# Base copies behind the weight loads, splits in another order in the first and last retention heads, and one vector's modulation summed as a stationary operand

## The chip, the cores and the metric

The kernel runs on one core of one Trainium2 chip. The metric is the device time of one execution in microseconds, as the median of the runs. Five engines work beside each other on the core: PE (TensorE, matrix products), DVE (VectorE), ACT (ScalarE), POOL (GpSimd) and SP (SyncE, which here only issues DMAs). Each engine takes its own instructions in the order in which they were written, and semaphores tie the engines together.

## The reference, cut to what matters

Two layers work on 512 latent tokens of width 1024, behind 256 context tokens. Layer 0 mixes the tokens with a gated MLP, layer 1 with bidirectional retention in four heads. Each is followed by a squared-ReLU MLP of width 4096. Every sub-layer is modulated by scale, shift and gate vectors, which are one product of a conditioning vector with `ada_w[i]`:

```python
mod_l = silu(c) @ ada_w[i] + ada_b[i]           # six vectors: sh1, s1, g1, sh2, s2, g2
h = x * (1 + s) + sh                            # per sub-layer
x = layernorm(alpha * x + g * f(h))

# layer 1's f: four heads, each with q, k, v and two gates from h @ b_w_in
s = gmlp; o_f, o_b = retention forward, retention backward (rope on q and k)
y = headnorm(o_f) * silu(g_f) + headnorm(o_b) * silu(g_b)
f(h) = y @ w_out
# the MLP: f(h) = square(relu(h @ w1)) @ w2
```

## The kernel before

**Precision and units.** The data is fp32. PE multiplies it as a sum of a high and a low part, with three matmuls per product (`hi*hi`, `lo*hi`, `hi*lo`; in the rows they are L1143, L1144, L1145, or L1181 to L1183 in the heads). Weights come in units of 128x1024 (512 KB). SP loads a unit into one of four `raw` slots (L911). ACT copies it to the high part (`split_hi`: L1799, L1842). DVE subtracts that from the unit to get the low part (`split_lo`: L2325, L2456). Then PE uses both. SP's load into a slot waits until DVE's split of the unit that lay in the slot is done (`done(n)`, a wait on `lo_done`), so a split that comes later on DVE also makes a later load.

**Phases.** Layer 0's mixer is followed by its MLP: ffn0a, six trips of ffn0 (p = 0 to 5), and ffn0z, the last piece. Then come the layer norm ln0b, three heads (`heads`), the last head (`headz`), ln1a, and the MLP of layer 1 (ffn1a, ffn1, ffn1z), which ends with ln1b. The MLPs and the heads' gate products use sums of weight blocks (`T1` to `T4`). For a head they are made in DRAM: SP copies a block there (`base`, L941, 1 MB each), and POOL adds another to it with an accumulating DMA (`gate_sum`, L3499). T2 adds T1's sum, so it waits for that; T4 adds T2's.

**The end of ffn0z.** While PE does the last blocks of the MLP, SP issues the lnbc loads, the four base copies for head 0, and the raw loads of the first head's units 0 to 3. ACT splits units 0 and 1, and then copies `rows` out of PSUM (`mod_rows`, L1945). `rows` is the sum over partitions of the modulation's products (`macc`), which the DVE accumulated: `mod_sums` (L1335) sums it with four matmuls of `ones`, and gives rows; `mod_columns` (L1345) transposes the copied rows with three matmuls, and DVE adds the bias (`mod1_columns`). PE can't go past `mod_columns` before ACT's copy is done. The gate row is then stored to DRAM from `modc` (L827) and loaded again (L834), and the raw loads for head 0's next units stand behind that on SP. POOL adds the MLP's blocks to the residual (L3409), and then shifts it with four accumulating DMAs (`shift_by_dma0`, L3451).

**The first head.** Beside its own units it makes the sums of the activations for the gate products: DVE `gx` (`operand1_sum`, L3136 and others), ACT the high parts `s_gs`, `pa_hi`, `s_y`, `pa_lo` (`operand1_hi`, L2146), DVE the low parts (`operand1_lo`, L3142). ACT's first of them also waits for POOL's four shifts. PE needs the units 6 and 7 split meanwhile.

**The end of headz.** Four `y` blocks (t = 3 to 0) are normed on DVE (L2369 to L3345), transposed on PE (L1636), copied by ACT as a high part (L2263) and by DVE as a low part (`y_low`, L3323), and multiplied with the units OUT to OUT+3. DVE then adds each product to the residual (L2692). The units of ffn1a's start are split in the same stretch (its unit 1 is `in_v`, its unit 2 `in_scr`).

## Time and profile before

| | us |
|---|---|
| median of 3 runs | 1962.84 |
| lowest and highest run | 1961.87, 1963.0 |
| the profiled execution | 1963.9 |
| its span in the trace | 1962.1 |
| PE busy | 1929.5 (98% of the span) |
| DVE busy | 1368.7 (70%) |
| ACT busy | 673.4 (34%) |
| POOL busy | 384.8 (20%) |

The mean granted clock of PE over the span is 0.995 of full speed. Busy times overlap; only the time in which PE has nothing to do, or runs slower, can be taken off without removing matmuls. In the views below a timeline row is start, duration, engine, line, operation, `out<-in`, and in brackets the idle time before it with what ended it.

### The profile page before, as it was taken

The numbers are of one execution on the slowest core, as the hardware profiler recorded it, in microseconds if no ns is written. First come the engines' busy times: TensorE is split into PE (matmuls) and PEld (weight loads), VectorE is DVE, ScalarE is ACT, GpSimd is POOL, SyncE is SP. The second block draws the span as 40 slices with busy tenths as digits, with TensorE's granted clock in tenths as the row PEclk, the third lists the DMA queues.
The fourth block names the chain that finished last, engine by engine and source line by source line (L and its number), as shares of the span: only waits on it lengthen the run. The fifth ranks groups of instructions, "written<-read, shape, count | busy, mean of one in ns | idle before, by whom it ended". The sixth has DMA issues, their size and how long they took to land.

```text
span 1962.1 us, 24859 instructions
## 1 busy us (share of the span) xinstructions
PE 1929.5 (98%) x9429; PEld 1651.9 (84%) x9429; DVE 1368.7 (70%) x1972; ACT 673.4 (34%) x930; POOL 384.8 (20%) x364
## 2 busy tenths in 40 slices
PE   9999999999999999999699999999999999999998
PEld 6889889889889988899587888888888878888887
DVE  3756678688778776777577744753754687777778
ACT  3423222234323322232246324423423444444443
POOL 0400311322221222112320130030030026100004
PEclk9999999999999999999899999999999999999999
DMA  9613334235998999988666366446447425886646
GB/s 329 256 65 75 109 122 129 94 119 150 204 250 208 222 225 220 241 229 209 191 155 218 127 200 194 155 158 205 169 133 240 161 86 172 236 220 188 181 143 149
DMA packets 120275, 350.07 MB, mean 178 GB/s; under 512 B 17504, under 2 KB 30432, under 8 KB 115424
## 3 DMA queue, kind: packets, MB, share of 16 engines
q1 hardware_dynamic: 91056, 267.58, 39.5%
q0 software_dynamic: 27280, 77.08, 21.8%
q10 hardware_dynamic: 1824, 3.85, 0.6%
q8 instruction: 75, 1.23, 0.3%
q14 instruction: 40, 0.33, 0.1%
HBM read 295.49 MB, written 39.87 MB: 171 GB/s over the span
## 4 chain that ended last, share of the span: by engine, by line
PE 89%; DVE 4%; DMA 3%; issue 1%; ACT 1%; POOL 1%; SPq 0%; POOLq 0%; DVEq 0%; ACTq 0%
PE bank L1143 17%; PE bank L1145 17%; PE bank L1144 17%; PE bank L1181 4%; PE bank L1183 3%; PE bank L1182 3%; PE bank L1544 3%; PE bank L1547 3%; PE bank L1546 3%; PE bank L1591 2%; PE bank L1594 2%; PE bank L1593 2%; PE bank L1776 2%; PE bank L1775 2%; PE bank L1773 2%; DMA raw<-w_units_d 2%
## 5 line engine op out<-in xcount | busy, mean ns | idle before, releaser
L2325 DVE TENSOR_TENSOR w_lo<-raw,w_hi 128x1024 fp32r<-128x1024 f32 x132 | 168.8, 1281 | 190.2 <-ACT w_hi L1799 189.9
L1799 ACT ACTIVATE w_hi<-raw 128x1024 fp32r<-128x1024 f32 x132 | 139.2, 1055 | 296.6 <-PE bank L1145 159.7
L1143 PE MATMUL bank<-w_hi,act_hi 128*128 128x512 f32 x504 | 198.3, 394 | 0.0
L1145 PE MATMUL bank<-w_hi,act_lo 128*128 128x512 f32 x504 | 196.5, 390 | 0.0
L1144 PE MATMUL bank<-w_lo,act_hi 128*128 128x512 f32 x504 | 196.3, 390 | 0.0
L1143 PE MATMUL bank<-hT_hi,w_hi 128*128 128x384 f32 (+2 forms) x544 | 192.2, 353 | 0.0
L1144 PE MATMUL bank<-hT_lo,w_hi 128*128 128x384 f32 (+2 forms) x544 | 190.9, 351 | 0.0
L1145 PE MATMUL bank<-hT_hi,w_lo 128*128 128x384 f32 (+2 forms) x544 | 190.8, 351 | 0.0
L1181 PE MATMUL bank<-w_hi,hT_hi 128*128 128x512 f32 x336 | 131.3, 391 | 2.0 <-DVE w_lo L2325 2.0
L3382 POOL TENSOR_TENSOR rstd<-veps,tiny 128x1 f32<-128x1 f32 x58 | 38.7, 666 | 471.6 <-DVE veps L2378 471.6
L1182 PE MATMUL bank<-w_lo,hT_hi 128*128 128x512 f32 x336 | 130.8, 389 | 0.0
L1183 PE MATMUL bank<-w_hi,hT_lo 128*128 128x512 f32 x336 | 130.8, 389 | 0.0
L3392 POOL TENSOR_TENSOR res_lat<-res_lat,gy 128x512 f32<-128x512 f32 x56 | 78.6, 1430 | 207.7 <-DVE gy L2434 207.6
L1143 PEld LDWEIGHTS bank<-w_hi,act_hi 128*128 128x128 f32 x504 | 94.6, 188 | 24.4 <-issue 5.4
L1145 PEld LDWEIGHTS bank<-w_hi,act_lo 128*128 128x128 f32 x504 | 94.6, 188 | 20.0
L1144 PEld LDWEIGHTS bank<-w_lo,act_hi 128*128 128x128 f32 x504 | 94.7, 188 | 18.9
L1143 PEld LDWEIGHTS bank<-hT_hi,w_hi 128*128 128x128 f32 x544 | 102.4, 188 | 9.0 <-issue 0.2
L1144 PEld LDWEIGHTS bank<-hT_lo,w_hi 128*128 128x128 f32 x544 | 102.4, 188 | 8.9 <-issue 0.2
L1145 PEld LDWEIGHTS bank<-hT_hi,w_lo 128*128 128x128 f32 x544 | 102.3, 188 | 8.4
L1842 ACT ACTIVATE w_hi<-raw 128x1024 fp32r<-128x1024 f32 x46 | 48.6, 1056 | 134.1 <-PE bank L1145 116.6
L1807 ACT ACTIVATE act_hi<-stage 128x384 fp32r<-128x384 f32 x96 | 50.4, 526 | 115.6 <-DVE stage L2518 61.3
L2456 DVE TENSOR_TENSOR w_lo<-raw,w_hi 128x1024 fp32r<-128x1024 f32 x46 | 56.2, 1222 | 36.9 <-ACT w_hi L1842 36.9
(447 smaller groups left out, 4859.7 us busy)
## 6 DMA issues: line engine op xcount, KB each, us to landing
raw<-w_units_d SPq DMA_DIRECT2D x234, 512.0 KB, 4.6
mod<-mod_units_d SPq DMA_DIRECT2D x64, 384.0 KB, 4.4
wsum<-w_units_d SPq DMA_DIRECT2D x45, 512.0 KB, 4.6
raw<-weight_sums_d SPq DMA_DIRECT2D x32, 512.0 KB, 4.3
wsum<-w_units_d POOLq DMA_DIRECT2D x26, 512.0 KB, 8.3
wsum<-wsum POOLq DMA_DIRECT2D x19, 512.0 KB, 6.9
bv<-mod_units_d SPq DMA_DIRECT2D x16, 512.0 KB, 3.7
weight_sums_d<-w_units_d POOLq DMA_DIRECT2D x8, 1024.0 KB, 14.3
```

Source lines behind the costliest of these rows:

```text
L1143: nc.tensor.matmul(out, s_hi, m_hi, start=first, stop=False)
L1144: nc.tensor.matmul(out, s_hi, m_lo, start=False, stop=False)
L1145: return nc.tensor.matmul(out, s_lo, m_hi, start=False, stop=last)
L1181: nc.tensor.matmul(bank[t][:, :], hT_hi[:, kc, tt], hi[:, c], start=kc == 0, stop=False)
L1182: nc.tensor.matmul(bank[t][:, :], hT_hi[:, kc, tt], lo[:, c], start=False, stop=False)
L1183: last = nc.tensor.matmul(bank[t][:, :], hT_lo[:, kc, tt], hi[:, c], start=False, stop=kc == KC - 1)
L1544: nc.tensor.matmul(out, hi[:, w], x_hi[:, kc, :], start=opens and kc == 0, stop=False, skip_group_check=True)
L1546: nc.tensor.matmul(out, hi[:, w], x_lo[:, kc, :], start=False, stop=False, skip_group_check=True)
L1547: last = nc.tensor.matmul(out, lo[:, w], x_hi[:, kc, :], start=False, stop=kc == KC // 2 - 1, skip_group_check=True)
L1799: nc.scalar.activation(halves_of(phase, k, i)[0], raw[:, s, :], ACT.Copy).then_inc(hi_done, 1)
L2325: tt(lo, raw[:, s, :], f32(hi), ALU.subtract).then_inc(lo_done, 1)
L3392: gt(r, r, gy[:, e % 2, :], ALU.add).then_inc(res_added, 1)
```

## The change

It has four parts.

1. **Order on SP and POOL at the end of ffn0z.** The four base copies are issued behind the raw loads of units 0 to 3 and not ahead of them, and POOL's sums T1 and T3 stand behind the additions to the residual.
2. **Columns at once.** For the trips p = 3, 4 and 5 of ffn0, `column_sums` takes a 128x128 block of `macc` as the stationary operand and two columns of ones as the moving one, three matmuls for each of two blocks. The result is already a column, so the four matmuls of `mod_sums` and the three transposes are left out. ACT copies 6 columns in place of 384, and DVE adds two halves.
3. **The first head.** Units 6 and 7 are split earlier among the activation sums, on ACT and DVE.
4. **The last head.** DVE splits OUT to OUT+2 between the `y` blocks and not in one run ahead of the gates, OUT+3 and ffn1a's unit 0 behind the last `y` block. ACT's copies are reordered to match.

```diff
                     sp.wait_ge(pe_step, step_of("ffn0z", 0, "q3.1"))
                     load_lnbc(lnbc0, 2)
-                    for x, block in ((T1, "B11"), (T3, "B12"), (T2, "B22"), (T4, "B21")):
-                        base(0, x, block)
                 done(7)
                 if more:
...
                 else:
                     load(at + 8 + 3, 3)
+                    for x, block in ((T1, "B11"), (T3, "B12"), (T2, "B22"), (T4, "B21")):
+                        base(0, x, block)
                 mods(4)
                 mods(5)
...
 
+                def column_sums(label, b, block):
+
+                    free(phase, i, label)
+                    for j in range(3):
+                        at = (3 * block + j) * P
+                        last = nc.tensor.matmul(bank[b][:, 2 * j:2 * j + 2], sum1(p)[:, at:at + P], ones[:, 0:2],
+                                                start=True, stop=True)
+                    last.then_inc(pe_step, 1)
+
                 def rows():
                     pe.wait_ge(mod_used, len(MOD1_SEQ) if phase == "ffn0z" else MOD1_SEQ.index((p, KC - 1)) + 1)
+                    if phase == "ffn0" and p >= PIECES_MIXED:
+                        column_sums("rows0", 6, 0)
+                        return
                     mod_sums(phase, i, "rows0", 6, [sum1(p), sum1(PIECES_F - 1 if phase == "ffn0z" else p, 1)],
                              WIDE_M1 // 2)
...
                     block0_hi(p, 10)
                     block0_hi(p + 1, 0)
-                    mod_rows(phase, i, 0, rows1[:, :], 6, begin)
+                    if p > PIECES_MIXED:
+                        act.wait_ge(dve_drain, drained(phase, i - 1, "cols0")[1])
+                    mod_rows(phase, i, 0, rows1[:, 0:6] if p >= PIECES_MIXED else rows1[:, :], 6, begin)
                     block0_hi(p + 1, 1)
                 else:
                     act.wait_ge(stage_full, count("full", phase, i, 2 + d))
                     stage_split(phase, i, 4 + d, k_hi[:, d, 0:TOKL], TOKL)
                 for k in range(6, 9):
-                    if first and k < 8:
-                        operand1_hi(2 * k - 12)
-                        operand1_hi(2 * k - 11)
+                    if first:
+                        for n in ((0,), (1,), (2, 3))[k - 6]:
+                            operand1_hi(n)
                     split_hi(phase, i, k, used_unit(phase, i, k - 2))
 
                 act.wait_ge(dec_in, h * 16 + 48)
...
                 if phase == "heads":
                     split_hi(phase, i, OUT, used_unit(phase, i, OUT - 2))
                 else:
-                    for k in range(OUT, OUT + 3):
-                        split_hi(phase, i, k, step_of(phase, i, "g2.1"))
-                    split_hi(phase, i, OUT + 3, used_unit(phase, i, OUT - 2))
+                    split_hi(phase, i, OUT, step_of(phase, i, "g2.1"))
                 gate(2, "g4.0")
                 gate(3, "g4.1")
                 if phase == "heads":
                     split_hi(phase, i, OUT + 1, used_unit(phase, i, OUT - 1))
                 else:
-                    split_hi("ffn1a", 0, 0, used_unit(phase, i, OUT - 1))
+                    for k in range(OUT + 1, OUT + 3):
+                        split_hi(phase, i, k, step_of(phase, i, "g2.1"))
+                    split_hi(phase, i, OUT + 3, used_unit(phase, i, OUT - 2))
                 for t in reversed(range(LAT)):
                     act.wait_ge(pe_step, step_of(phase, i, f"y{t}"))
                     nc.scalar.activation(act_hi1[:, :, t * P:(t + 1) * P],
                                          bank[4 + t][:, :].rearrange("p (a b) -> p a b", a=CH), ACT.Copy)\
                         .then_inc(psum_hi, 1)
+                    if phase == "headz" and t == 3:
+                        split_hi("ffn1a", 0, 0, used_unit(phase, i, OUT - 1))
                     if phase == "headz" and t == 1:
                         split_hi("ffn1a", 0, 1, step_of(phase, i, "ob0"))
                 if phase == "headz":
...
-            EARLY = {"gmlpz": ("ffn0a", 0, 1), "ffn0z": ("heads", 0, 2), "headz": ("ffn1a", 0, 2)}
+            EARLY = {"gmlpz": ("ffn0a", 0, 1), "ffn0z": ("heads", 0, 2), "headz": ("ffn1a", 0, 1)}
...
+                    if phase == "headz" and n == 1:
+                        split_lo("ffn1a", 0, 2)
                     if n < LAT + 1:
                         drain_block(phase, 2 * n, order)
                     second_half(phase, n - 1, ln_phase)
...
+                    if i >= PIECES_MIXED:
+                        dve.wait_ge(act_drain, drained(phase, i, "rows0")[1])
+                        tt(out[:, 0], rows1[:, 0:6].rearrange("p (j v) -> p j v", v=2), bias[:, 0], ALU.add)
+                        tt(out[:, 1], bank[7][:, 0:6].rearrange("p (j v) -> p j v", v=2), bias[:, 1], ALU.add)\
+                            .then_inc(dve_drain, 1)
+                        return
                     src = bank[7][:, 0:3 * P].rearrange("p (j b v r) -> p b j v r", j=3, b=2, v=2)
...
                 for d in range(2):
                     stage_lo_part(phase, i, 4 + d, k_lo[:, d, 0:TOKL], k_hi[:, d, 0:TOKL], TOKL)
-                if first:
-
-                    operand1_sum(gx21, gx11, gx21)
                 split_lo(phase, i, 6)
                 if first:
+
+                    operand1_sum(gx21, gx11, gx21)
                     operand1_lo(0)
                     operand1_lo(1)
+                    split_lo(phase, i, 7)
 
                     operand1_sum(gx11, gx22, gx11)
 
...
@@ -3308,15 +3336,10 @@
                 gate_c22(1)
                 decayed(1, 12, 10, backward, range(3, 6),
                         {3: (lambda: of_gated(2),), 4: (13, lambda: of_gated(3))})
-                if phase == "headz":
-                    for k in range(OUT, OUT + 3):
-                        split_lo(phase, i, k)
                 gate_c21(0)
                 gate_c21(1)
-                if phase == "headz":
-                    split_lo(phase, i, OUT + 3)
-                else:
-                    split_lo(phase, i, OUT)
+                split_lo(phase, i, OUT)
+                if phase == "heads":
                     split_lo(phase, i, OUT + 1)
                 def y_low(t):
                     dve.wait_ge(psum_hi, h * 10 + (TILES0 + LAT - t))
@@ -3344,10 +3367,13 @@
                     dve.wait_ge(dve_drain, drained(phase, i, f"ob{t}")[1])
                     stt(y[:, t, :], rbuf[:, n % 2, :], rstd[:, 4 + t:5 + t], y[:, t, :], ALU.mult, ALU.add)\
                         .then_inc(y_step, 1)
-                    if phase == "headz" and t == 3:
-                        split_lo("ffn1a", 0, 0)
+                    if phase == "headz":
+                        if t > 1:
+                            split_lo(phase, i, OUT + LAT - t)
+                        elif not t:
+                            split_lo(phase, i, OUT + 3)
                 if phase == "headz":
-                    split_lo("ffn1a", 0, 1)
+                    split_lo("ffn1a", 0, 0)
                 y_low(0)
...
                 nc.gpsimd.dma_start(weight_sums_d[h, x], other, accum_op=ALU.add, max_dma_last_dim=8192)\
                     .then_inc(t_sum0[x], 16)
 
-            gate_sum(0, T1)
-            gate_sum(0, T3)
             for t in range(TILES0):
                 pool.wait_ge(gy_added[t], 16 * 2 * (PIECES_F - 1))
             add_blocks("ffn0z", "ln0b", 2 * TILES0)
-            gate_sum(0, T2)
+            for x in (T1, T3, T2):
+                gate_sum(0, x)
             shift_by_dma0("ln0b", LAT)
             gate_sum(0, T4)
             pool.wait_ge(shifted0, 16 * (TILES0 + LAT))
```

**SP, at the end of ffn0z.** `raw` is a weight slot, `weight_sums_d` the four base copies. Before:

```order
179 L838 DMA lnbc<-ln_d 128x1024
180 L839 DMA lnbc<-ln_d 128x1024
181 L941 DMA weight_sums_d<-w_units_d 16x16384 x4
182 L911 DMA raw<-w_units_d 128x1024 x4
183 L1004 DMA rope<-rope_d 128x1024
184 L827 DMA gate_rows_d<-modc 128x8x1 x2
```

After the change:

```order
179 L838 DMA lnbc<-ln_d 128x1024
180 L839 DMA lnbc<-ln_d 128x1024
181 L911 DMA raw<-w_units_d 128x1024 x4
182 L941 DMA weight_sums_d<-w_units_d 16x16384 x4
183 L1004 DMA rope<-rope_d 128x1024
184 L827 DMA gate_rows_d<-modc 128x8x1 x2
```

The four raw loads stand ahead of the four base copies; the rope load and the store of the gate row stay behind both.

**DVE, in the first head.** The first row is the split of the head's keys, `w_lo` are the units 6, 7 and 8. Before:

```order
793 L2334 TENSOR_TENSOR k_lo<-stage,k_hi 128x512 x2
794 L3136 TENSOR_TENSOR gx<-gx 128x1024
795 L2325 TENSOR_TENSOR w_lo<-raw,w_hi 128x1024
796 L3142 TENSOR_TENSOR s_gs<-gx,s_gs 128x1024
797 L3142 TENSOR_TENSOR pa_hi<-gx,pa_hi 128x1024
798 L3136 TENSOR_TENSOR gx<-gx 128x1024
799 L3204 TENSOR_TENSOR gx<-gx,hT_hi 128x1024
800 L3206 TENSOR_TENSOR gx<-gx,hT_lo 128x1024
801 L2325 TENSOR_TENSOR w_lo<-raw,w_hi 128x1024
802 L3142 TENSOR_TENSOR s_y<-gx,s_y 128x1024
803 L3142 TENSOR_TENSOR pa_lo<-gx,pa_lo 128x1024
804 L2325 TENSOR_TENSOR w_lo<-raw,w_hi 128x1024
```

After the change:

```order
796 L2354 TENSOR_TENSOR k_lo<-stage,k_hi 128x512 x2
797 L2345 TENSOR_TENSOR w_lo<-raw,w_hi 128x1024
798 L3164 TENSOR_TENSOR gx<-gx 128x1024
799 L3170 TENSOR_TENSOR s_gs<-gx,s_gs 128x1024
800 L3170 TENSOR_TENSOR pa_hi<-gx,pa_hi 128x1024
801 L2345 TENSOR_TENSOR w_lo<-raw,w_hi 128x1024
802 L3164 TENSOR_TENSOR gx<-gx 128x1024
803 L3232 TENSOR_TENSOR gx<-gx,hT_hi 128x1024
804 L3234 TENSOR_TENSOR gx<-gx,hT_lo 128x1024
805 L3170 TENSOR_TENSOR s_y<-gx,s_y 128x1024
806 L3170 TENSOR_TENSOR pa_lo<-gx,pa_lo 128x1024
807 L2345 TENSOR_TENSOR w_lo<-raw,w_hi 128x1024
```

Unit 6 is split ahead of the first `gx`, and unit 7 ahead of the last three.

**ACT, at the end of headz.** `xw_hi` are the units OUT to OUT+2, the next `w_hi` is OUT+3, then come ffn1a's unit 0 (`w_hi`), unit 1 (`in_v_hi`) and unit 2 (`in_scr_hi`), and the four copies of `y` (`pa_hi<-bank`). Before:

```order
577 L2214 ACTIVATE gs<-bank 128x512 x2
578 L1799 ACTIVATE xw_hi<-raw 128x1024 x3
579 L1799 ACTIVATE w_hi<-raw 128x1024
580 L2209 ACTIVATE gs<-gs 128x512 x2
581 L1799 ACTIVATE w_hi<-raw 128x1024
582 L2263 ACTIVATE pa_hi<-bank 128x4x128 x3
583 L1799 ACTIVATE in_v_hi<-raw 128x1024
584 L2263 ACTIVATE pa_hi<-bank 128x4x128
585 L1799 ACTIVATE in_scr_hi<-raw 128x1024
```

After the change:

```order
578 L2232 ACTIVATE gs<-bank 128x512 x2
579 L1814 ACTIVATE xw_hi<-raw 128x1024
580 L2227 ACTIVATE gs<-gs 128x512 x2
581 L1814 ACTIVATE xw_hi<-raw 128x1024 x2
582 L1814 ACTIVATE w_hi<-raw 128x1024
583 L2281 ACTIVATE pa_hi<-bank 128x4x128
584 L1814 ACTIVATE w_hi<-raw 128x1024
585 L2281 ACTIVATE pa_hi<-bank 128x4x128 x2
586 L1814 ACTIVATE in_v_hi<-raw 128x1024
587 L2281 ACTIVATE pa_hi<-bank 128x4x128
588 L1814 ACTIVATE in_scr_hi<-raw 128x1024
```

Only OUT is copied ahead of the gates; ffn1a's unit 0 is behind the first copy of `y`, its unit 1 still ahead of the last copy of `y`.

## Rows read from the trace of the kernel before

**Rows 1.** What PE waited for, whole span: us in total, times, longest

```profile
PE bank L1345 <- ACT rows L1945: 16.6, 1, 16.6
PE bank L1636 <- DVE y L3345: 2.4, 2, 1.9
```

**Rows 2.** Timeline of PE around the wait at the end of ffn0z

```profile
943.65 0.39 PE L1145 MATMUL bank<-xw_hi,act_lo 128*128 128x512 f32 x1
960.67 0.90 PE L1345 MATMUL bank<-ident,rows 128*128 128x128 f32 x3 [16.63 <-ACT rows L1945]
...
982.94 1.10 PE L1363 MATMUL bank<-ident,res_lat 128*128 128x128 f32 x8
```

**Rows 3.** A window in the wait: length, busy of each engine (instructions), clock, DMA share, GB/s

```profile
950.00:960.00 10.00, 0.00 (x0) 0.00 (x0) 1.23 (x1) 1.87 (x2) 0.00 (x0) 0.50 1.01 282
```

**Rows 4.** Timeline of PE, the same program stretch in gmlpz

```profile
426.94 0.60 PE L1345 MATMUL bank<-ident,vtok 128*128 128x128 f32 x4
...
446.71 1.09 PE L1363 MATMUL bank<-ident,res_lat 128*128 128x128 f32 x8
```

**Rows 5.** Timeline of ACT at the end of the wait

```profile
959.18 1.06 ACT L1799 ACTIVATE in_s_hi<-raw 128x1024 fp32r<-128x1024 f32 x1 [4.54 <-DMA raw<-w_units_d]
960.15 0.47 ACT L1945 ACTIVATE rows<-bank 128x384 f32<-128x384 f32 x1
```

**Rows 6.** Timeline of SP's DMA issues

```profile
929.70 2.51 SPq L941 DMA_DIRECT2D weight_sums_d<-w_units_d  x4
933.16 8.31 SPq L911 DMA_DIRECT2D raw<-w_units_d  x4
...
964.30 1.06 SPq L827 DMA_DIRECT2D gate_rows_d<-modc  x2
980.86 0.33 SPq L834 DMA_DIRECT2D gate_lat<-gate_rows_d  x1
...
1040.51 0.38 SPq L1028 DMA_DIRECT2D raw<-weight_sums_d  x1
```

**Rows 7.** Landing times of the four raw loads issued from 933.2 to 941.1

```profile
DMA to landing us min/median/max: 20.4/20.7/22.3
```

**Rows 8.** Page, section 6: KB each, us to landing

```profile
raw<-w_units_d SPq DMA_DIRECT2D x234, 512.0 KB, 4.6
```

**Rows 9.** Landing times of the raw load issued at 1569.7

```profile
DMA to landing us min/median/max: 3.5/3.5/3.5
```

**Rows 10.** Landing times of weight_sums_d DMAs issued from 925 to 945

```profile
DMA to landing us min/median/max: 7.3/13.8/18.3
```

**Rows 11.** Timeline of PE around trip 3's sums and transposes

```profile
767.95 0.85 PE L1335 MATMUL bank<-macc,ones 128*32 128x384 f32 x8
...
771.60 0.49 PE L1345 MATMUL bank<-ident,rows 128*128 128x128 f32 x3
```

**Rows 12.** Timeline of PE at the start: dcol stationary, two columns moving

```profile
46.01 0.95 PE L1325 MATMUL bank<-dcol,rbuf 128*128 128x2 f32 x8
```

**Rows 13.** Timeline of PE in the first head

```profile
1037.85 0.50 PE L1181 MATMUL bank<-w_hi,hT_hi 128*128 128x512 f32 x1 [1.30 <-DVE w_lo L2325]
...
1047.06 0.50 PE L1181 MATMUL bank<-w_hi,hT_hi 128*128 128x512 f32 x1 [0.72 <-DVE w_lo L2325]
```

**Rows 14.** Timeline of ACT in the first head

```profile
1032.54 1.04 ACT L2146 ACTIVATE s_gs<-gx 128x1024 fp32r<-128x1024 f32 x1
```

**Rows 15.** Timeline of DVE at the end of headz

```profile
1598.46 0.74 DVE L3345 SCALAR_TENSOR_TENSOR y<-rbuf,rstd,y 128x512 f32<-128x512 f32 x1
```

**Rows 16.** Timeline of ACT at the end of headz

```profile
1596.13 1.05 ACT L1799 ACTIVATE in_v_hi<-raw 128x1024 fp32r<-128x1024 f32 x1
```

**Rows 17.** Timeline of PE at the end of headz

```profile
1615.84 1.09 PE L1363 MATMUL bank<-ident,res_lat 128*128 128x128 f32 x8
```

**Rows 18.** Timeline of POOL: T2's sum, the fourth shift of the residual

```profile
993.80 0.96 POOL L3499 DMA_DIRECT2D weight_sums_d<-weight_sums_d  x1
...
1026.32 0.86 POOL L3451 DMA_DIRECT2D res_lat<-lnbc  x1 [10.15 <-issue]
```

More of the change, by code:

```diff
@@ L1556, in columns @@
                 def columns():
+                    if phase == "ffn0" and p >= PIECES_MIXED:
+                        column_sums("cols0", 7, 1)
+                        return
                     mod_columns(phase, i, 0, rows1, 7)
@@ L1898, in ffn0 @@
                     split_hi("heads", 0, 1, step_of(phase, i, "q3.1"))
+                    act.wait_ge(dve_drain, drained("ffn0", p - 1, "cols0")[1])
                     mod_rows(phase, i, 0, rows1[:, :], 6, begin)
@@ L3012, in mod1_columns @@
                     bias = bias.unsqueeze(3).to_broadcast([P, 2, 3, 2])
+                    if i >= PIECES_MIXED:
[3 more added lines that the diff above has]
+                            .then_inc(dve_drain, 1)
+                        return
                     src = bank[7][:, 0:3 * P].rearrange("p (j b v r) -> p b j v r", j=3, b=2, v=2)
@@ L3192, in head @@
                     stage_lo_part(phase, i, 4 + d, k_lo[:, d, 0:TOKL], k_hi[:, d, 0:TOKL], TOKL)
+                split_lo(phase, i, 6)
                 if first:
                     operand1_sum(gx21, gx11, gx21)
-                split_lo(phase, i, 6)
-                if first:
                     operand1_lo(0)
                     operand1_lo(1)
+                    split_lo(phase, i, 7)
                     operand1_sum(gx11, gx22, gx11)
@@ L3206, in head @@
                     tt(kcs(gx22[:, :]), kcs(gx22[:, :]), f32(hT_lo[:, second, g_first]), ALU.add).then_inc(s_sum0, 1)
-                split_lo(phase, i, 7)
-                if first:
                     operand1_lo(2)
                     operand1_lo(3)
+                else:
+                    split_lo(phase, i, 7)
                 split_lo(phase, i, GATE)
```

## The prediction

> **What bounds the kernel now.** I read first what PE waited for over the whole span [rows 1], because PE is busy almost throughout and little else can be won. One wait stands out: 16.6 us, once, in front of the transposes of `rows` (L1345), released by ACT's copy. The next two are small: 2.4 us in two waits for `y` in the last head (the longer 1.9), and two waits for a low split in the first head are 1.30 and 0.72 us [rows 13].
>
> Then the timeline around the large wait [rows 2]. The last matmul before it starts at 943.65 and the transposes at 960.67, which is 17.02 us from start to start, where the matmuls before stood 0.23 us apart: 16.8 us are lost. The window in the wait [rows 3] shows PE at nothing, DVE with a single 1.23 us instruction, ACT at 1.87 us, and the DMA engines fully in use (share 1.01, 282 GB/s): the engines wait for transfers. It shows the granted clock at 0.50, which is 1.2 of 2.4 GHz, and the matmuls go on at that for a while after the wait. What this costs can be read from two stretches with the same program, the down blocks up to the first transposes of the residual: here 982.94 - 960.67 = 22.27 us [rows 2], in gmlpz 446.71 - 426.94 = 19.77 us [rows 4]. The difference, 2.5 us, belongs to the wait too.
>
> What is the copy late for? ACT copies `rows` at 960.15, right behind its split `in_s_hi` of unit 1, and that had waited 4.54 us for its `raw` load and started at 959.18 [rows 5]. SP shows why the load landed so late [rows 6]: four base copies of 1 MB were issued at 929.70 and the raw loads from 933.16 on, so that unit 1 lay behind 4 MB. Those four raw loads landed 20.4 to 22.3 us after their issue [rows 7]. The raw loads of the whole kernel land in a median of 4.6 us [rows 8], one alone in 3.5 us [rows 9]. The base copies and the sums made from them took from 7.3 to 18.3 us [rows 10], and nobody on SP needs a sum before 1040.51 [rows 6].
>
> **Part 1, the order on SP and POOL.** The raw loads are now issued ahead of the base copies. SP issues the four from 933.16 over 8.31 us [rows 6], held only by the slots; so that of unit 1 goes out at about 937 and lands at 941 (3.5 us) to 942 (4.6 us). Unit 0 is there before ACT gets to it. ACT then splits unit 1 in 1.06 us and copies `rows` in 0.47 us [rows 5]: done at about 943.2, where PE wants it at 943.65 + 0.23 = 943.88. The wait goes, with 0.7 us to spare, and with it the slow clock: 16.8 + 2.5 = 19.3 us. Against it I set 0.3 us: the DVE split that ran inside the wait [rows 3] now falls among the drains of the down blocks (nothing at best, its whole 1.23 us at worst). **Gain 19.0 us.**
>
> What is late next? Each step behind the base copies on SP's queue. The rope load and the stores of the gate row stand behind them in order. Before, the stores were issued at 964.30 and the load that waits for them went out at 980.86 [rows 6], 16.6 us later. After, they are issued some 17 us earlier, but find the base copies still under way; I put them in DRAM at 971 to 973, which is 8 to 10 us earlier than before while PE is 19 us earlier, so 9 to 11 us of slack are used up. The gate row is needed only by the head's gated sums, some 20 us on, and the next four raw loads behind it on SP are for units 4 and on. I take this as covered; if the cover is gone, each microsecond costs one. POOL's sums T1 and T3 go behind its additions, and T2 behind them, from 993.80 [rows 18] - 19.3 = 974.5 on: even at 18.3 us each [rows 10] T1, then T2, land by about 1011, and SP's first use stands at 1040.51 - 19.3 = 1021 [rows 6]. Hidden.
>
> **Part 2, the columns.** Three trips lose four summing matmuls (8 records, 0.85 us) and three transposes (0.49 us), 1.34 us [rows 11], and get two times three matmuls with two moving columns. The nearest row is that of `dcol` with two columns, 8 records in 0.95 us [rows 12]; so six records cost 0.71 us, twice 1.43 us. That is 0.09 us more per trip, **a loss of 0.2 us** in all. At the price of a transpose, 0.49 / 3 = 0.16 us [rows 11], the six cost 0.98 and 1.1 us are gained; at the price of a whole `dcol` group for each half, 1.90, 1.7 us are lost. The smaller copy on ACT and the second addition on DVE are not on the path in ffn0: PE stands there for neither [rows 1].
>
> **Part 3, the first head.** PE waited for the low splits of units 6 and 7 at 1037.85 (1.30 us) and 1047.06 (0.72 us) [rows 13]; both waits are followed by a slow first matmul (0.50 us), and from start to start I count 1.46 and 0.88 us lost. ACT's `s_gs` copy starts at 1032.54 [rows 14], and unit 6's split stands behind the next copy, which itself waits for a `gx`. With unit 6 directly behind `s_gs`, ACT has it at 1034.6 and DVE's low part, 1.23 us as in [rows 3], is there at 1035.8, where PE is ready at 1037.85 - 1.46 = 1036.4. Unit 7 is split before the last three `gx` operations and is ready at about 1040.4, over 4 us ahead of need. The sums that are pushed back by one split each are used after unit 8. **Gain 2.3 us**; 0 if the margin of 0.6 us is used up by something else.
>
> **Part 4, the last head.** The three low splits ahead of the gates go between the `y` blocks; so the waits for `y`, 2.4 us in all [rows 1], should go. But the low split of OUT+3 now stands behind the last `y` block on DVE. Before, that block's end was at 1598.46 + 0.74 = 1599.2 [rows 15]; without the waits it is at about 1596.8. Then come the split (1.2 us), only then SP's load of ffn1a's unit 1 (3.5 us, [rows 9]), and ACT's `in_v_hi` (1.05 us, [rows 16]), which stands ahead of the last copy of `y` on ACT: 1596.8 + 1.2 + 3.5 + 1.05 = 1602.6. Before, `in_v_hi` was already split at 1596.13 and that copy could start at 1599.2 + 0.6 = 1599.8. So the last copy comes 2.8 us later, the products ahead of it on PE 2.4 us earlier. Before, the stretch ended with the transposes at 1615.84 [rows 17]; it ends between 2.4 us earlier and 2.8 us later. The two nearly cancel: **a loss of 0.3 us**.
>
> **The sum** is -19.0 + 0.2 - 2.3 + 0.3 = -20.8 us. Durations come from the execution of 1963.9 us, which would become 1943.1; it lies 1.1 us above the median of 1962.84, and the median becomes 1942.0 us.
>
> **Rivals.** *(a) Only part of the wait goes.* The raw loads still meet the first base copies on the engines. If unit 1's took what loaded transfers took, 7.3 us at the least and 13.8 in the median [rows 10], it landed at 944.3 or 950.8, the copy of `rows` 1.6 us later, and PE waited 2.0 or 8.5 us. With up to 1.5 us of slow clock that leaves a total of 18.8 or 10.8 us: 1944 to 1952, in the middle 1948. The 4.6 us of the other loads [rows 8] speak against it.
>
> *(b) The transfers aren't ordered.* If the base copies and the raw loads share the engines whatever their order of issue, unit 1 lands as before and only the small parts are left: -1.8 us, 1961.0, no change that can be told. Against it: the raw loads behind the base copies took 20.4 us or more [rows 7], those elsewhere 4.6 [rows 8].
>
> *(c) POOL's sums hold up its shifts.* T2's issue waits for T1, and the four shifts stand behind it. T1 is issued where T2 was at 993.80 [rows 18], less 19.3: 974.5 + 18.3 = 993 lets the first shift out just where it would be, and the fourth, at 1026.32 before [rows 18], is due at 1007. If sums took twice as long beside busy engines (36.6 us), T2 went out at 1011, the fourth shift at 1016 instead of 1007, and ACT's `s_gs` in the first head, which waits for it, would hold unit 6 back by about 8 us: total 13 us, 1950. For it: two sums of the base copies took up to 18.3 us while DVE stood nearly still [rows 10], so a busy DVE has not been seen with them there.
>
> The Trainium skill ("DMA: Bandwidth & Descriptors", section SWDGE vs HWDGE vs iDMA) speaks for it: the descriptor rings of DMAs that GpSimd issues lie in SBUF, where DVE can lock GpSimd out in its two-port mode. No run here shows such a lock. By it the time would be that of (c).
>
> *(d) Slower.* The same mechanism carried further: the gain is eaten up when T2 lands so late that the first head's sum unit comes 20.8 us late, that is after 1021 + 20.8 = 1042, and slower by 0.2% from 1046. T1 and T2 issued from 974.5 would have to take 71 us together; at 18.3 us each they take 37 [rows 10].
>
> *(e) The last head goes one way.* If the load of ffn1a's unit 1 lands in 4.6 us or more, the copy of the last `y` is later still: +2.5 in place of +0.3, total 18.6, 1944.2. If PE's products ahead cover all of it, -2.4: total 23.5, 1939.3.
>
> **How the numbers follow.** The forecast with (e) on both sides has 0.80, (a) 0.06, (c) 0.06, (b) 0.04, (d) 0.02, and 0.02 is for a gain beyond 24 us. A measurement of this kernel tells about 0.2%, 3.9 us, from no change. Faster: 0.80 + 0.06 + 0.06 + 0.02 = 0.94; same: (b), 0.04; slower: (d), 0.02. The range reaches from (e)'s better end, 1939.3, less 0.5 us for the spread of the runs, to the middle of (a), and leaves out half of (a), (b), (c), (d) and the larger gain, less than 0.2 in all: 1938.8 to 1948.0.
>
> **What would show it.** Right: no wait at L1345 in ffn0z, a granted clock of 1.00 through that stretch, raw loads landing in 3 to 5 us there, 19.8 us from the column transposes to the residual's first transposes; no wait for units 6 and 7; in headz no wait for `y`, but one for the last `y_low`, with ACT's `in_v_hi` waiting for DMA. Wrong: a new PE wait in the first head with ACT's `s_gs` released by a DMA, or DVE waiting for the gate row. The step most likely to be off in size is part 4.

## The result, and the profile after

The changed kernel takes 1943.64 us (median of 6 runs, 1941.41 to 1946.51), the kernel before 1963.42 us (6 runs, 1961.87 to 1966.47). The ratio is 0.9899, with a 95% interval of [0.9886, 0.9912]: 19.8 us faster, where 20.8 were forecast. The profiled execution took 1941.41 us, its span is 1939.6 us, and it is the fastest of the six.

The waits of PE in the changed kernel, over the whole span, answer to [rows 1]:

```profile
PE bank L1363 <- ACT res_lat L1976: 2.0, 1, 2.0
PE bank L1143 <- DVE pa_lo L3346: 1.8, 2, 1.4
PE bank L1317 <- DMA mod<-mod_units_d: 1.5, 4, 0.6
PE bank L1418 <- POOL tiny L3489: 1.3, 1, 1.3
```

The wait for `rows` (16.6 us) and those for `y` are gone, and no wait for a low split in the first head is left. Two new ones are in the last head: for the low part of `y` (`pa_lo`) and for the normed residual (`res_lat`). The other two rows stood in the kernel before too, with 0.5 and 1.3 us. The next view is PE's timeline at the places of [rows 2], the transposes of `rows` and the first transposes of the residual:

```profile
942.48 0.49 PE L1345 MATMUL bank<-ident,rows 128*128 128x128 f32 x3
...
962.16 1.09 PE L1363 MATMUL bank<-ident,res_lat 128*128 128x128 f32 x8
```

These are 19.68 us apart, where they were 22.27. The window over the former wait answers to [rows 3]; its columns are the same:

```profile
940.00:950.00 10.00, 10.00 (x47) 8.28 (x46) 8.46 (x15) 4.50 (x5) 6.05 (x5) 1.00 1.10 406
950.00:960.00 10.00, 10.00 (x46) 8.29 (x45) 7.57 (x18) 2.49 (x2) 7.95 (x8) 1.00 0.69 158
```

PE is at 10.00 of 10.00 us and the granted clock at 1.00. SP and ACT show why, as in [rows 5] and [rows 6]. First SP's issues, then ACT:

```profile
931.79 8.32 SPq L911 DMA_DIRECT2D raw<-w_units_d  x4
940.15 2.55 SPq L941 DMA_DIRECT2D weight_sums_d<-w_units_d  x4
...
945.07 7.39 SPq L827 DMA_DIRECT2D gate_rows_d<-modc  x2
968.04 0.33 SPq L834 DMA_DIRECT2D gate_lat<-gate_rows_d  x1
```

```profile
938.95 1.06 ACT L1814 ACTIVATE in_s_hi<-raw 128x1024 fp32r<-128x1024 f32 x1
939.92 0.47 ACT L1963 ACTIVATE rows<-bank 128x384 f32<-128x384 f32 x1
```

The four raw loads, which landed 20.4 to 22.3 us after their issue [rows 7], landed in

```profile
DMA to landing us min/median/max: 3.4/3.5/4.3
```

ACT's `in_s_hi` has no wait ahead of it, and the copy of `rows` is done at 939.92 + 0.47 = 940.4, 2.1 us before PE gets to the transposes.

To see where the time went in each part, I compared the start of the same PE instruction in the two traces:

| PE instruction | before | after | difference |
|---|---|---|---|
| behind the column step of trip 5 | 898.26 | 896.59 | -1.67 |
| transposes of `rows` in ffn0z | 960.67 | 942.48 | -18.19 |
| first transposes of the residual | 982.94 | 962.16 | -20.78 |
| unit 6 of the first head | 1037.85 | 1015.62 | -22.23 |
| unit 7 of the first head | 1047.06 | 1023.78 | -23.28 |
| transposes of y3 in headz | 1587.70 | 1563.69 | -24.01 |
| transposes of y1 | 1594.98 | 1568.70 | -26.28 |
| first product with the last y | 1604.69 | 1580.19 | -24.50 |
| transposes of the residual | 1615.84 | 1593.34 | -22.50 |

The first 1.7 us belong to no part of the change: 0.7 us arise in the first 35 us and 1.0 us at one wait at 532.8, in code that it does not touch, and such steps of either sign stand in every trace below. The end of ffn0z gives 19.4 us (the difference just ahead of it was -1.38), the first head 2.5, and headz first 3.0 and then takes 3.8 back. That is 21.1 us in this pair of executions, of which the medians of all runs show 19.8.

### The profile page after: what moved, and what is told of

It is laid out like the page before. It is cut to its first block, busy times and chain, and to the rows that moved or that the text cites. A ratio compares the mean times of both kernels' runs of the same rounds, so it can differ in the third digit from the quotient of the medians.

```text
span 1939.6 us, 24868 instructions
## 1 busy us (share of the span) xinstructions
PE 1924.6 (99%) x9432; PEld 1652.1 (85%) x9432; DVE 1368.7 (71%) x1975; ACT 672.5 (35%) x930; POOL 382.8 (20%) x364
## 3 DMA queue, kind: packets, MB, share of 16 engines
q8 instruction: 75, 1.23, 0.2%
## 4 chain that ended last, share of the span: by engine, by line
PE 92%; DVE 2%; DMA 2%; issue 1%; POOL 1%; SPq 1%; ACT 1%; POOLq 0%; DVEq 0%; ACTq 0%
PE bank L1143 17%; PE bank L1144 17%; PE bank L1145 17%; PE bank L1181 4%; PE bank L1182 4%; PE bank L1183 4%; PE bank L1544 3%; PE bank L1547 3%; PE bank L1546 3%; PE bank L1608 3%; PE bank L1609 3%; PE bank L1606 3%; PE bank L1790 2%; PE bank L1788 2%; PE bank L1791 2%
## 5 line engine op out<-in xcount | busy, mean ns | idle before, releaser
L1181 PE MATMUL bank<-w_hi,hT_hi 128*128 128x512 f32 x336 | 131.0, 390 | 0.0
L1144 PEld LDWEIGHTS bank<-w_lo,act_hi 128*128 128x128 f32 x504 | 94.7, 188 | 18.8
```

The lines of the kernel that those rows point to most:

```text
L1144: nc.tensor.matmul(out, s_hi, m_lo, start=False, stop=False)
L1181: nc.tensor.matmul(bank[t][:, :], hT_hi[:, kc, tt], hi[:, c], start=kc == 0, stop=False)
```

## The experiments

Each time is a median, each ratio is against runs of the kernel before on the same chip, and what a run gains or loses is worked out from its ratio. "In the trace" means by the starts of the same PE instructions, as in the table above.

**One part at a time.** *order_only* is the kernel before with the two hunks of part 1:

```diff
-  for x, block in (...): base(0, x, block)      # SP, ahead of the raw loads
+  for x, block in (...): base(0, x, block)      # SP, behind them
-  gate_sum(0, T1); gate_sum(0, T3)              # POOL, ahead of add_blocks
+  for x in (T1, T3, T2): gate_sum(0, x)         # POOL, behind it
```

> The kernel before with part 1 alone (raw loads ahead of the base copies on SP, POOL's sums T1 and T3 behind its additions). My theory: the whole wait of 16.6 us at L1345 goes and the slow clock behind it with it, so the two waits in the first head and the two in the last head stay as in the kernel before, and the time falls by 19.4 us (+-1), that is 0.990 of before. Rival: the four parts only bring this together (the splits in the first head are needed to use the earlier loads); then less than 16 us.

1945.83 us, ratio 0.9908 [0.9893, 0.9923]: 18.1 us faster. PE's waits at L1181 and L1636 are 2.0 and 2.7 us, about as before. In the trace the same stretch as above gives 19 us; of that, 1.4 us are lost again in the last head, where the clock fell behind the wait for `y` (see the last section). Part 1 works alone, and is nine tenths of the whole.

*first_only* is the kernel before with the hunks of the first head, of which ACT's is shown; DVE's splits move to match:

```diff
-  if first and k < 8: operand1_hi(2 * k - 12); operand1_hi(2 * k - 11)
+  if first:
+      for n in ((0,), (1,), (2, 3))[k - 6]: operand1_hi(n)
```

> The kernel before with part 3 alone (units 6 and 7 split earlier in the first head). My theory: the two waits for w_lo (1.30 and 0.72 us) go, 2.3 to 2.5 us less, everything else unchanged, the 16.6 us wait included. Rival: the split of unit 6 is early enough only because part 1 made the shifts earlier; then the first of the two waits stays and the gain is about 1 us.

1961.28 us, ratio 0.9988 [0.9979, 0.9997]: 2.4 us faster. PE's wait for `rows` is there with 16.9 us and both waits at L1181 are gone. Each of the two parts works without the other.

*last_only* is the kernel before with the hunks of headz alone, on DVE and on ACT:

```diff
-  for k in range(OUT, OUT + 3): split_lo(phase, i, k)      # ahead of the gates
+  if t > 1: split_lo(phase, i, OUT + LAT - t)              # between the y blocks
+  elif not t: split_lo(phase, i, OUT + 3)
```

> The kernel before with part 4 alone (the last head's splits between the y blocks). My theory: the waits for y go (2.4 us), but ACT stands 6 to 8 us on a raw load ahead of the last copy of y, PE waits for pa_lo and for the residual instead, and the sum is 0.5 to 1.0 us slower than before in the trace, which is too little for the clock of whole runs. Rival: the new waits are made by the other parts' earlier DMAs, then this alone is 2 us faster.

1965.71 us, ratio 1.0012 [1.0003, 1.0021]: 2.4 us slower, more than the 0.5 to 1.0 us expected. Its PE waits show the exchange, 2.4 us for `y` against 3.9 us for other things:

```profile
PE bank L1363 <- ACT res_lat L1958: 2.0, 1, 2.0
PE bank L1143 <- DVE pa_lo L3322: 1.9, 2, 1.5
```

The loss is larger than the difference of the waits. In the trace 3.1 us are gained at `y`, 3.9 are lost at the other waits, and 1.6 more right behind the wait of 2.0 us, where the granted clock stands at 0.50 (last column but two):

```profile
1616.00:1618.00 2.00, 2.00 (x7) 1.52 (x5) 1.91 (x7) 1.94 (x5) 1.06 (x2) 0.50 0.00 0
```

*columns_only* is the kernel before with `column_sums` and what belongs to it on ACT and DVE:

```diff
+  if phase == "ffn0" and p >= PIECES_MIXED:
+      column_sums("rows0", 6, 0)
+      return
```

> The kernel before with part 2 alone (three trips' sums by a stationary operand). My theory: 0.0 us, the two forms cost the same on PE to 0.1 us per trip. Rivals: 1.1 us faster if a small matmul costs a transpose's price, 1.7 us slower at the price of the dcol group.

1964.98 us, ratio 1.0005 [0.9996, 1.0014]: not told from no change. PE's start differences step by -0.30 us at each `rows` and by +0.30 us at each `cols`, in all three trips, and so cancel. The rows of the changed kernel for trip 3, against 0.85 and 0.49 us in [rows 11], are

```profile
766.17 0.72 PE L1556 MATMUL bank<-ones,macc 128*128 128x2 f32 x6
...
769.58 0.72 PE L1556 MATMUL bank<-ones,macc 128*128 128x2 f32 x6
```

**Why the loads were late.** *base_on_pool* takes the kernel before and changes only who issues the four base copies:

```diff
-  for x, block in (...): base(0, x, block)                        # SP
+  pool.wait_ge(pe_step, step_of("ffn0z", 0, "q3.1"))
+  for x, block in (...): nc.gpsimd.dma_start(weight_sums_d[0, x], w_units[k:k + 2])
```

> The kernel before, where only the queue of the four base copies for head 0 is another: POOL issues them, after the same step of PE, and SP's raw loads stay where they were. All four are waited for together before the first sum. If the raw loads were late because they stood behind 4 MB in one queue, they now share the engines with the copies and land in 6 to 14 us and not in 20 to 22, and the wait at L1345 shrinks from 16.6 to under 9 us. If the engines' rate was the cause, whatever the queue, unit 1 lands as late as before (20 us) and the wait stays above 14 us.

1956.14 us, ratio 0.9960 [0.9947, 0.9973]: 8 us faster. The raw loads, issued from 931.83 over 8.32 us as in the kernel after, land in

```profile
DMA to landing us min/median/max: 10.0/14.1/16.1
```

and PE waits 6.7 us for `rows`:

```profile
PE bank L1344 <- ACT rows L1944: 6.7, 1, 6.7
PE bank L1362 <- ACT res_lat L1957: 2.8, 1, 2.8
```

The wait is under the 9 us of the first theory. But two of the four loads took 15.7 and 16.1 us, more than its 6 to 14, and the run doesn't part the two causes as it was meant to. POOL's queue was free, and the copies went out much earlier there:

```profile
920.25 2.02 POOL L3507 DMA_DIRECT2D weight_sums_d<-w_units_d  x4 [8.13 <-PE bank L1546]
937.14 1.74 POOL L3501 DMA_DIRECT2D weight_sums_d<-w_units_d  x2 [14.88 <-DMA weight_sums_d<-w_units_d]
```

That is 11.6 us ahead of the raw loads and not 3.5. The four copies landed in

```profile
DMA to landing us min/median/max: 6.4/10.3/15.0
```

so the last, issued at 921.8, was in DRAM at 936.7, when SP had issued only the loads of units 0 and 1. The loads of units 2 and 3 ran beside POOL's two sums (from 937.14) alone, and were the slowest. What the run does show is that loads in a queue of their own are slow too, 10.0 to 16.1 us for 3.5, beside copies and then beside the sums. The Trainium skill ("DMA: Bandwidth & Descriptors", section Queues, rings and completion order) says that a DMA engine takes turns between its queue rows packet by packet. The landing times agree in that loads and sums moved together; how large a turn is, no run here shows.

The trace of the kernel before has POOL's sums in it too. Its four base copies alone landed in

```profile
DMA to landing us min/median/max: 7.3/11.1/15.9
```

so the last, issued at 931.6, was in DRAM at 947.5. The load of unit 1, issued at 936.9, took 22.3 us and landed at 959.2: 11.6 us after the last base copy, and 0.2 us after T3's sum, which POOL had issued at 940.6 and which took 18.3 us. About half of that load's time passed when no base copy was left, beside POOL's sums. Part 1 takes both out of the loads' way, and so does sp_only below, where the sums wait for the later copies. A run that moves POOL's sums alone and leaves the base copies ahead would part them. None was made, so how much of the 20 us belongs to the place behind the copies and how much to the sums stays open.

*sp_only* is part 1 without its POOL half:

```diff
-  for x, block in (...): base(0, x, block)      # SP, ahead of the raw loads
+  for x, block in (...): base(0, x, block)      # SP, behind them
```

> The kernel before with SP's half of part 1 alone; POOL still does T1's and T3's sums ahead of its additions to the residual. My theory: POOL now waits for base copies that are issued 10 us later and land at about 953 to 958, before it adds the first block at what was 942 to 943, so that the residual's norm is 10 to 15 us late; PE runs through its down blocks and then waits there: the wait at L1345 goes and another of 5 to 12 us comes, for the residual. Rival: POOL has room, then 19 us faster, as with both halves.

1952.04 us, ratio 0.9939 [0.9924, 0.9954]: 12 us faster, 6 us short of both halves. POOL's timeline shows it waiting for a base copy ahead of T1's and T3's sums, and its first additions to the residual at 952.95, where the changed kernel has them at 942.89:

```profile
949.30 0.90 POOL L3499 DMA_DIRECT2D weight_sums_d<-w_units_d  x1 [38.72 <-DMA weight_sums_d<-w_units_d]
952.39 0.83 POOL L3499 DMA_DIRECT2D weight_sums_d<-w_units_d  x1 [2.20 <-DMA weight_sums_d<-w_units_d]
952.95 2.79 POOL L3409 TENSOR_TENSOR res_lat<-res_lat,gy 128x512 f32<-128x512 f32 x2
```

PE waits, one step further on, for a drain that DVE can't do while its buffer is not added. The wait is 4.7 us, where 5 to 12 were expected, at the residual. PE comes out of it at the lower of the two levels of the clock and is back at the full one from 964 on (last column but two):

```profile
958.60 0.79 PE L1143 MATMUL bank<-xw_hi,act_hi 128*128 128x512 f32 x1 [4.68 <-DVE gy L2692]
```

```profile
957.00:963.00 6.00, 4.40 (x10) 3.46 (x11) 4.33 (x10) 2.27 (x2) 4.14 (x6) 0.50 1.00 227
964.00:970.00 6.00, 6.00 (x28) 4.94 (x27) 4.33 (x12) 1.27 (x2) 4.77 (x5) 1.00 0.99 142
```

**How much room is behind the loads.** *double_base* puts 4 MB more into the queue ahead of the base copies:

```diff
+  for n in range(4): sp.dma_start(spare_d[n], w_units[k:k + 2])
   for x, block in ((T1, "B11"), (T3, "B12"), (T2, "B22"), (T4, "B21")): base(0, x, block)
```

> The changed kernel with four more copies of 1 MB into a spare place, ahead of the four base copies. It tells what room there is behind the raw loads. My theory: the gate row's load and the sums are about 12 to 18 us later; the gate row had some 10 us of room, so DVE waits for it and the time rises by 0 to 8 us. If the room is larger than I think, no change (within 1 us); no theory gives a later raw load of units 0 to 3.

1954.48 us, ratio 0.9947 [0.9932, 0.9962]: about 9.4 us slower than the changed kernel by the two ratios, where 0 to 8 were expected. The load of the gate row went out at 986.86 and not at 968.04, and DVE waited for it:

```profile
998.36 0.17 DVE L3195 COPY tiny<-lg 128x2 f32<-128x2 f32 x1 [14.19 <-DMA gate_lat<-gate_rows_d]
```

In the changed kernel the same instruction runs at 982.89, and the load of the gate row, out at 968.04, took 4.7 us: it was there at 972.7, with 10 us to spare. Here it went out 18.8 us later and took 11.4. In the trace PE lost 7.6 us at the first head's start, 1.9 us more to the lower clock right behind that, and 2.2 us at the next units. For the gate row, the place behind the loads has room for 10 us and no more.

**The last head.** In the changed kernel ACT, then DVE and PE show the exchange there:

```profile
1568.65 1.06 ACT L1814 ACTIVATE w_hi<-raw 128x1024 fp32r<-128x1024 f32 x1 [3.73 <-DMA raw<-w_units_d]
...
1577.78 1.06 ACT L1814 ACTIVATE in_v_hi<-raw 128x1024 fp32r<-128x1024 f32 x1 [7.10 <-DMA raw<-w_units_d]
1578.74 0.58 ACT L2281 ACTIVATE pa_hi<-bank 128x512 fp32r<-128x512 f32 x1
```

```profile
1579.35 0.69 DVE L3346 TENSOR_TENSOR pa_lo<-bank,pa_hi 128x512 fp32r<-128x512 f32 x1 [3.96 <-ACT pa_hi L2281]
...
1583.57 1.69 DVE L2345 TENSOR_TENSOR in_scr_lo<-raw,in_scr_hi 128x1024 fp32r<-128x1024 f32 x1
```

```profile
1580.19 0.47 PE L1143 MATMUL bank<-xw_hi,pa_hi 128*128 128x512 f32 x1 [1.38 <-DVE pa_lo L3346]
...
1593.34 1.09 PE L1363 MATMUL bank<-ident,res_lat 128*128 128x128 f32 x8 [2.02 <-ACT res_lat L1976]
```

ACT stands 7.10 us on the raw load for `in_v_hi`, with the last copy of `y` behind it, and DVE's low part waits 3.96 us for that copy. *y_first* moves the two splits that wait for loads behind the copies:

```diff
-  if phase == "headz" and t == 3: split_hi("ffn1a", 0, 0, ...)
-  if phase == "headz" and t == 1: split_hi("ffn1a", 0, 1, ...)
+  if phase == "headz" and t == 1: split_hi("ffn1a", 0, 0, ...)
+  if phase == "headz" and t == 0: split_hi("ffn1a", 0, 1, ...)
```

> The changed kernel with ACT's copies of y ahead of the splits that wait for loads: ffn1a's unit 0 behind the copy of y1, unit 1 behind the copy of y0. My theory: DVE's low part of the last y no longer waits 3.96 us, PE's waits for pa_lo (1.8 us in two) go, and a part of the 2.0 us wait for the residual too: 2 to 4 us faster than the changed kernel, 22 to 24 us below the kernel before. Rival: the wait for the residual is bound by DVE's work between the drains, then only 0 to 1.5 us.

1941.16 us, ratio 0.9884 [0.9868, 0.9899]. Beside the trace of the changed kernel PE gains 0.4, 1.7 and 0.6 us at the two `pa_lo` waits and the residual's, 2.7 in all; both `pa_lo` waits are gone, and the residual's is left with 1.5 us. Repeated on another chip:

> The kernel y_first once more, beside the one above on the same chip: 0.988 of before, as the first time. It also shows whether the 0.9 us wait for unit 6 in the first head, which came with ACT 1.50 us on the fourth shift's DMA, comes in each execution; by my theory it does in some, since the fourth shift lands within 1 to 2 us of ACT's need.

1940.26 us, ratio 0.9887 [0.9870, 0.9904]. By the ratios the two lie 2.9 and 2.4 us below the changed kernel, but the intervals overlap: the place of the gain is shown, its size in whole runs is not settled. ACT's wait for the fourth shift was there in the first execution and not in the second:

```profile
1014.57 1.06 ACT L2164 ACTIVATE s_gs<-gx 128x1024 fp32r<-128x1024 f32 x1 [1.50 <-DMA res_lat<-lnbc]
```

```profile
1012.93 1.04 ACT L2164 ACTIVATE s_gs<-gx 128x1024 fp32r<-128x1024 f32 x1
```

*tail_late* is y_first with one more move, which goes after the rest of the residual's wait. DVE's splits of ffn1a's units 1 and 2 move later among the drains:

```diff
-  "headz": ("ffn1a", 0, 1)                                      # ahead of the second drain
-  if phase == "headz" and n == 1: split_lo("ffn1a", 0, 2)
+  if phase == "headz" and n < 3: split_lo("ffn1a", 0, n)
```

> The kernel y_first, and in it DVE splits ffn1a's units 1 and 2 later among the drains: unit 1 behind the second drain and the first statistics, unit 2 one block later. In y_first the wait for the residual at the end of headz (1.5 us) follows from two drains that PE had ready at about 1580.3 and 1583.0 and DVE did at 1581.7 and 1584.8, behind those splits. My theory: the wait shrinks to 0 to 0.3 us, 1.2 to 1.5 us faster than y_first. Rival: the splits move the delay to the second pair's norm or to ffn1a's first units, and the gain is 0 or a loss of 1 us.

1941.49 us, ratio 0.9884 [0.9868, 0.9900]: no gain, and the wait is longer (1.5 us in y_first):

```profile
1593.30 1.16 PE L1363 MATMUL bank<-ident,res_lat 128*128 128x128 f32 x8 [2.15 <-ACT res_lat L1976]
```

My theory had picked the wrong pair. The first block's norm on ACT did come 1.4 us earlier (1586.23), but PE's transposes need the second block's, and the split of unit 2 now stood ahead of that. *tail_later* moves this one two blocks on:

```diff
-  if phase == "headz" and n < 3: split_lo("ffn1a", 0, n)
+  if phase == "headz" and n in (1, 3): split_lo("ffn1a", 0, (n + 1) // 2)
```

> The kernel tail_late, with DVE's split of ffn1a's unit 2 two blocks later again (behind the fourth block's first statistics). In tail_late the first pair's norm came 1.4 us earlier, but PE's transposes wait for the second block's norm, and the split of unit 2 (1.93 us beside POOL's addition) stood right ahead of that. My theory: with it gone the norm on ACT starts at 1590 and not at 1592.0, PE's wait falls from 2.1 us to 0.4 or less and the slow clock that followed it in tail_late does not come: 2 to 3 us faster than tail_late, 1 to 2 us faster than y_first. Rival: the split delays the third and fourth block's norm by as much, and PE waits there instead; then no change against y_first.

1942.11 us, ratio 0.9890 [0.9873, 0.9906]. PE's waits there:

```profile
1593.77 1.10 PE L1363 MATMUL bank<-ident,res_lat 128*128 128x128 f32 x8 [0.38 <-ACT res_lat L1976]
...
1604.24 1.94 PE L1363 MATMUL bank<-ident,res_lat 128*128 128x128 f32 x16 [0.96 <-issue]
```

The first wait fell to 0.38 us as expected, by the starts 1.2 us less than in y_first, and 1.1 us came back at the fourth block's transposes: the rival held. DVE is full there (4.93 of 5 us from 1595 to 1600), so its splits can be moved but not hidden. *columns_back* is the changed kernel itself, beside it on the same chip.

> The changed kernel itself once more, beside the one above on the same chip and with the same runs of the kernel before: 0.990 of before. tail_later should be below it by 3 to 5 us; by the rival by 2 to 3 us.

1945.29 us, ratio 0.9905 [0.9888, 0.9921]; tail_later is 3.2 us below it, no more than y_first is below the changed kernel.

## Why the prediction was right

**Part 1** was right in mechanism and size: 19.4 us in the trace for 19.0. PE is at full clock throughout, the raw loads land in 3.4 to 4.3 us for the 3.5 to 4.6 assumed, and 19.68 us for 19.8 pass to the residual's transposes. The 0.3 us set against it for DVE did not come in the changed kernel, which is most of the difference between 19.4 and 19.0. The copy of `rows` was done with 2.1 us to spare and not 0.7: the load of unit 1 was there before ACT was free, and the forecast had taken it at its late bound. One thing in it was narrower than what happened. The prediction gave the place behind 4 MB as the reason for the late loads, but half of the time of unit 1's load passed after the last base copy, beside POOL's sums, and base_on_pool shows that loads in a queue of their own are slow too. That the change moved the sums as well covered this, and the forecast of the time did not depend on it. The text also did not say that POOL's half is needed; sp_only puts a price of 6 us on it.

**What is late next**: nothing, as forecast. The gate row was in DRAM at 968.0, where 971 to 973 were forecast. The sums T1 and T3 were issued at 972.93 and T2's at 983.15 (974.5 and 993 forecast, on the clock of a trace 1.7 us later), the first shift at 992.24, the first use of a sum at 1018.97.

**Part 2** was forecast as a loss of 0.2 us and is 0.0: a group of six takes 0.72 us, as worked out, but what counts is the time to the next matmul, 0.58 and 0.59 us here, and by that the two forms are equal.

**Part 3**: 2.5 us for 2.3; both waits are gone in the changed kernel. Alone, 2.4 us.

**Part 4** was the term that was mis-sized: 0.3 us of loss forecast, 0.8 in the trace (3.0 gained at the `y` waits, 3.8 lost behind them), and 2.4 us in runs of it alone, of which 1.6 in its trace are the slow clock. The end lay between the bounds of 2.4 us earlier and 2.8 later, and the last copy of `y` came when worked out: it starts at 1578.74, which with the 23.3 us won until then is 1602.0 for the 1602.6 forecast. What failed is the step that takes this copy for the only late thing. Of the 3.8 us, 1.5 are the wait for it. The split `w_hi` of ffn1a's unit 0 waited 3.73 us for its load at 1568.65 with the copy of y2 behind it, and PE lost 0.3 us there. The remaining 2.0 us are the wait for the residual, which the sum did not have: DVE's row of splits behind the last `y`, with two more among the drains, made the norm late. y_first and tail_later bear this out. With the copies of `y` ahead of the splits 2.7 us come back, so that part 4 would have been a gain of 1.9 us in the trace, and the residual's wait goes to 0.38 us when DVE's splits move.

**Rival (c)**, sums that hold up POOL's shifts, is there in small. ACT's wait for the fourth shift is 0 in the changed kernel, columns_back, y_first_again and tail_late, but 1.50 us in y_first and 2.41 us in tail_later, and PE then waits 0.9 and 1.8 us for unit 6. The rows of POOL's third and fourth shift, first in the changed kernel, then in y_first:

```profile
994.51 0.87 POOL L3477 DMA_DIRECT2D res_lat<-lnbc  x1 [0.25 <-issue]
1006.07 0.86 POOL L3477 DMA_DIRECT2D res_lat<-lnbc  x1 [10.69 <-issue]
```

```profile
998.92 0.87 POOL L3477 DMA_DIRECT2D res_lat<-lnbc  x1 [3.45 <-issue]
1009.63 0.86 POOL L3477 DMA_DIRECT2D res_lat<-lnbc  x1 [9.84 <-issue]
```

PE was only 1.2 us behind in y_first, the fourth shift 3.6. The landing times say what held it. T2's sum landed at 994.1 in the changed kernel, before the third shift's turn, and at 998.6 in y_first, and the third shift went out 0.3 us after that. The fourth goes out 0.3 us after the third has landed in every trace of this case. So the forecast's path was right, with sums that took a little longer (T1 11.3 us for 9.6, T2 12.6 for 11.0) and not twice as long. Why POOL issues a shift only then, and why the sums took longer in two executions, is not shown.

The rest of the distance to the forecast, 1 us in the median, is within the spread of the runs. The slow clock behind the residual's wait, 1.6 us in columns_back and absent in the profiled execution of the changed kernel, is of that size.

## What to carry to other kernels

Put a bulk copy that nobody needs soon behind the small loads that somebody needs next, in time and not only in another queue (there it still slowed them, 10.0 to 16.1 us for 3.5). Move the transfers that build on it with it, and look whether another engine (here POOL) waits for the copy in the middle of its own work. An in-order engine should do what is ready before what waits for a load: a copy of PSUM that stands behind a split waiting for DRAM is as late as the load. When a wait is to be taken away, read first which of several equal steps (here which block's norm) releases it.

## What the runs showed of the hardware

**The clock falls, or doesn't, after the same short wait.** The changed kernel waited 2.02 us for the residual in one execution, 1.98 in another. In the first the granted clock stayed at 1.00 and in the second it fell. First the window of the one, the changed kernel's, then that of the other, columns_back:

```profile
1590.00:1600.00 10.00, 7.99 (x52) 6.85 (x51) 8.69 (x20) 6.11 (x13) 6.11 (x6) 1.00 0.12 29
```

```profile
1596.00:1600.00 4.00, 4.00 (x16) 3.32 (x16) 3.13 (x8) 2.54 (x6) 2.21 (x3) 0.57 0.00 0
```

Matmuls at the lower of the two levels (1.2 GHz) stood 0.43 us apart and not 0.23, for some eight of them: 1.6 us, nearly as much as the wait. PE had stood still for the same time before. The wait for `y` gives a second pair: 1.92 us in the kernel before, with a clock of 1.00 behind it, and 1.92 us in order_only, with 0.50 from 1578 to 1580 and 1.4 us lost. The executions of one kernel can differ by such pieces.

**DVE and POOL take turns at SBUF.** DVE's low split takes 1.22 us nearly everywhere, but 1.95 in y_first at the end of headz, started while POOL adds a block (in the changed kernel, above, 1.69 at the same place):

```profile
1582.91 1.95 DVE L2345 TENSOR_TENSOR in_scr_lo<-raw,in_scr_hi 128x1024 fp32r<-128x1024 f32 x1
```

```profile
1582.48 1.30 POOL L3435 TENSOR_TENSOR res_lat<-res_lat,gy 128x512 f32<-128x512 f32 x1 [2.58 <-DVE gy L2712]
```

POOL's addition ends at 1583.78, and the split 1.08 us later, at 1584.86: as if all but its first 0.14 us had been done only then. The same is in tail_late, where POOL's addition ends at 1588.16 and the split of 1.93 us at 1589.24. In the changed kernel 19 of the 268 splits of this kind take 1.30 us or more, and each ends 1.08 to 1.09 us after an operation of POOL. It goes the other way too: there a split that starts at 942.75 takes its 1.23 us, and POOL's addition, started at 942.89, takes 2.25 us for 1.29. The Trainium skill ("SBUF — State Buffer", section SBUF: two separate sides) says that a DVE operation with two SBUF inputs and a GpSimd operation lock the port pair that they share for a whole instruction each, and whichever starts first has it. These traces agree for POOL's operations of two inputs, with 0.7 us lost in each of the first two meetings. They don't for POOL's operations of one input: beside one that runs from 65.50 to 68.29 a split from 66.59 on took 1.23 us.
